# A hand-cut plan of front work over 256 gather groups: new cuts for the early units, and a later due time for a tile's second four heads

## The chip, the cores and the metric

The kernel runs on one core of one Trainium2 chip. The metric is the device time of one execution in microseconds (us), the median of several runs; lower is better.

## The reference, cut to what matters

One layer of a decoder serves a prompt of 1024 rows (8 tiles of 128 rows) and a sample of 8 rows, all in float32. For every row the reference computes

```
h = rmsnorm(x) @ w_in                      # latents, rotary key, three conv inputs
o = softmax(mask(q . k)) @ ckv             # 4 heads, causal; the sample attends to 2048 paged rows
x1 = x + concat(norm(o @ w_uv), norm(conv)) @ w_o
xn2 = rmsnorm(x1)
q = xn2 @ w_query                          # 8 heads x 2 halves x 128
16 best of 128 keys in each half, 16 best of the 256 sums, softmax -> gates, expert numbers
y = rmsnorm(x1 + sum over 128 slots of gate * gelu(xn2 . expert_u[slot]) * expert_v[slot])
```

The last line is the heavy one: each row has 8 x 16 = 128 slots, and each slot wants one row of 4 KB of `expert_u` and one of `expert_v`, fetched by its own number.

## The kernel before, in words

**The stream of groups.** The 128 slots of a tile are served four at a time, so a tile has 32 groups and the 8 prompt tiles have 256. For each slot POOL issues one indirect DMA into `u_ring` and one into `v_ring` (L1853, 128 rows of 4 KB each). Both rings hold 8 slots, which is two groups. In group g, VectorE (DVE) multiplies gelu by the gate (`weigh_group`, L1742) and then takes the four dot products of group g+1 (`dot_group`, L1736); ScalarE (ACT) builds four small diagonal matrices (`diag_group`, L1222) and the gelu of group g+1 (L1215); TensorE (PE) multiplies them with `v_ring` into `acc` (`v_group`, L924, 16 matmuls of 512 columns). A dot product frees its slot of `u_ring`, the matmuls of L924 free theirs of `v_ring`, and only then may POOL gather into that slot again (`gather_group`, L1856). POOL takes the groups in fixed order: the four u gathers of group g+1, the four v gathers of group g.

**The front work.** Everything else (projections, attention, the output projection with `mix_out`, the norms, the queries and the picks of the experts) is cut into named stages. It is done by units: unit 0 is tile 0, unit 1 is tile 1, units 2, 3 and 4 are the pairs of tiles 2 and 3, 4 and 5, 6 and 7, and unit 5 is the sample. The front work of unit 0 runs before the first group; the front work of each later unit runs beside the groups of the tiles before it. `front_of(u)` is projections, attention, feed-forward norm and the query of the first four heads with their `select`; `rest_of(u)` is the query of the last four heads with theirs; in a pair the picks of the second tile are taken later, by `second_picks(u)` (8 `tops` and 2 `select`).

**The plan.** `make_plan` (L178) takes segments (first group, end, list of stages) and lays the stages of a segment over its groups in proportion to the hand-written `COST` (L160). Three engines read the plan: in group g PE does its part of the stages and then `v_group(g)`; DVE does `weigh_group(g)`, `dot_group(g+1)` and then its part of the stages; ACT does `diag_group(g)`, `gelu_group(g+1)` and then its part. In a group with `pages` stages (the sample's attention) the order is a little different: PE puts only the first stage ahead of `v_group`, and DVE puts two of its four dots behind the first stage. POOL and SP don't read the plan: their orders are fixed, and their waits on semaphores follow the stages. SP loads the weights of the stages piece by piece (1 MB each, a ring `w_ring` of two pieces), the tiles of x, and the pages of the sample's cache (32 DMAs for each of 8 samples, double-buffered; the load of one sample waits until the matmuls with the values of the one before the last are done).

**Due times.** `make_plan` asserts that a `select` of tile f lies where a pick buffer is free and before group 32 f - 1. What POOL really waits for (L1856) is finer: the picks of a tile's first four heads before its first group, the picks of the second four heads before its group 16.

Of the kernel before, what the change touches and what calls it, by code (L numbers as in the profile page):

```python
# [44 lines left out]
TOPK = 16  # L45
# [18 lines left out]
G = 4  # L64
GROUPS = SLOTS // G
# [9 lines left out]
SAMPLE = len(UNITS) - 1  # L75
PICK_BUFS = 3
# [17 lines left out]
def parts_of(u):  # L94

    return [(0, 1), (1, 2), (2, 4), (4, 8)] if u == 0 else [(0, 4), (4, 8)]
# [23 lines left out]
def project_stages(u):  # L120

    n = len(UNITS[u])
    return ([(name, i) for i in range(n) for name in ("norm", "turn")] + [("latent", k) for k in range(3)] + [("z_in", 0), ("latent_norm", 0), ("z_in", 1)]
            + [("z_gate", k) for k in range(2)] + [("conv", 0), ("latent_scale", 0), ("conv", 1)] + [("kv_rows", i) for i in range(n)])


def mix_stages(u):

    if u == 0:
        return [(name, 0) for name in ("q_proj", "q_latent", "first_heads", "attn", "first_mix", "first_ffn", "ffn_turn")]  # L130
    stages = []
    for i in range(len(UNITS[u])):
        stages += [("q_proj", i), ("q_latent", i)]
        stages += [("pages", n) for n in range(SB * QUARTERS + QUARTERS)] if u == SAMPLE else [("head", (i, h)) for h in range(H + 1)]
        stages += [("attn", i), ("mix_norm", i)]
    return stages + [("mix_out", k) for k in range(N_OUT)] + [(name, i) for i in range(len(UNITS[u])) for name in ("ffn_norm", "ffn_turn")]


def pick_stages(u, part):

    stages = [("query", 0)] if part == 0 else []
    return stages + [("query", h + 1) for h in range(*parts_of(u)[part])] + [("select", (part, 0))]


def second_picks(u):

    return sum([[("tops", h) for h in range(*heads)] + [("select", (part, 1))] for part, heads in enumerate(parts_of(u))], [])


def front_of(u):  # L150

    return project_stages(u) + mix_stages(u) + pick_stages(u, 0)


def rest_of(u):

    return sum([pick_stages(u, part) for part in range(1, len(parts_of(u)))], [])
# [10 lines left out]
def cost(u, name, n):  # L168

    if name == "head":  # L170
        return 3.5 + 1.2 * UNITS[u][n[0]]
    if name == "select":
        h0, h1 = parts_of(u)[n[0]]
        return 5 + 3 * (h1 - h0)
    return COST[name] * (1.6 if len(UNITS[u]) > 1 and name in SHARED else 1)


def make_plan(segments):  # L178

    groups = [[] for g in range(TILES * GROUPS)]  # L180
    for first, end, stages in segments:
        total, done = sum(cost(*s) for s in stages), 0.0
        for u, name, n in stages:
            g = first + int(done * (end - first) / total)
            if name == "select" and u != SAMPLE:
                f = UNITS[u][n[1]]
                assert f == 0 or max(0, (f + 1 - PICK_BUFS) * GROUPS + 2) <= g < f * GROUPS - 1, (f, g)
            groups[g].append((u, name, n))
            done += cost(u, name, n)
    return [groups[it * GROUPS:(it + 1) * GROUPS] for it in range(TILES)]  # L190
# [16 lines left out]
def of_unit(u, stages):  # L207

    return [(u, name, n) for name, n in stages]


PLAN = make_plan([(0, 30, of_unit(0, rest_of(0)) + of_unit(1, front_of(1) + rest_of(1))),
                  (30, 62, of_unit(2, front_of(2) + rest_of(2))),
                  (62, 74, of_unit(2, second_picks(2))),
                  (74, 120, of_unit(3, front_of(3) + rest_of(3))),
                  (120, 132, of_unit(3, second_picks(3))),
                  (132, 181, of_unit(4, front_of(4) + rest_of(4))),
                  (181, 193, of_unit(4, second_picks(4))),
                  (193, 250, of_unit(SAMPLE, front_of(SAMPLE) + rest_of(SAMPLE) + [("sample_picks", 0)]))])
LAST = TILES - 1  # L220


def has_pages(stages):
    return any(name == "pages" for u, name, n in stages)
# [36 lines left out]
def build(nc, a, out):  # L261

    with ExitStack() as ctx:
# [313 lines left out]
        def _(pe):  # L577
# [407 lines left out]
            def tile(it):  # L985

                for g, stages in enumerate(PLAN[it]):
                    ahead = 1 if has_pages(stages) else len(stages)
# [57 lines left out]
        def _(act):  # L1046
# [210 lines left out]
            def tile(it):  # L1257
                for g, stages in enumerate(PLAN[it]):
                    late = has_pages(stages)
                    if g:  # L1260
                        diag_group(it, g)
                    if g and not late and g + 1 < GROUPS:
                        gelu_group(it, g + 1)
                    if g == GROUPS - 2 and not late and it < LAST:
                        load_xn2(it + 1)
                    for s in stages:
                        stage(own, *s)
                    if g and late and g + 1 < GROUPS:
                        gelu_group(it, g + 1)
                    if g == GROUPS - 2 and late and it < LAST:  # L1270
                        load_xn2(it + 1)
                    if g == X1_GROUP:
                        load_x1(it)
# [31 lines left out]
        def _(dve):  # L1305
# [464 lines left out]
            def tile(it):  # L1770
                for g, stages in enumerate(PLAN[it]):

                    half = G // 2 if has_pages(stages) else G
                    if g:
                        weigh_group(it, g)
                    if g and g + 1 < GROUPS:
                        dot_group(it, g + 1, 0, half)
                    ahead = 1 if has_pages(stages) else len(stages)
                    for s in stages[:ahead]:
                        stage(own, *s)  # L1780
                    if g and g + 1 < GROUPS:
                        dot_group(it, g + 1, half, G)
                    for s in stages[ahead:]:
                        stage(own, *s)
# [167 lines left out]
```

## Time and profile before

| | us |
|---|---|
| median of 3 runs | 3503.11 (3503.08 to 3503.35) |
| the profiled execution | 3499.09 |
| its span, first to last instruction | 3497.3 |
| busy: PE / DVE / ACT / POOL | 2499.0 / 2279.7 / 812.6 / 2290.4 |
| mean granted TensorE clock | 0.842 of full speed |
| bytes moved by DMA, rate over the span | 1279.47 MB, 366 GB/s |

The profile is read by stretches of groups. The start of a group is the start of its multiply of L1742 on DVE. In this trace group 0 starts at 150.2 us, group 8 at 262.5, group 30 at 567.2, group 62 at 1040.4, group 74 at 1181.8, group 120 at 1759.1, group 132 at 1901.6, group 181 at 2524.1, group 193 at 2664.4, group 201 at 2773.2 and group 231 at 3167.8. So 567.2 to 1040.4 is the segment of unit 2's main work (32 groups), 1181.8 to 1759.1 that of unit 3 (46 groups), 1901.6 to 2524.1 that of unit 4 (49 groups), and 2664.4 to 3167.8 the sample's projections and pages. An idle time with an arrow, `<-`, names what ended it.

### The profile page before, as it was taken

How to read it: one execution, taken by the hardware profiler on the slowest of the kernel's cores; microseconds unless marked ns; L12 is line 12 of the kernel's file. 1: busy time of each engine (PE TensorE's matmuls, PEld its weight loads, DVE VectorE, ACT ScalarE, POOL GpSimd, SP SyncE). 2: the span in 40 equal slices, each digit the busy share in tenths (PEclk: the TensorE clock that was granted, in tenths of full speed). 3: DMA queues.
4: the chain of work that ended last, by engine and by line, in shares of the span. 5: the costliest groups of instructions: out<-in, count | busy, mean ns of one | idle time of the engine just before them, and what ended most of it. 6: DMA issues, size and time to landing. Idle time of an engine off the chain costs nothing.

```text
span 3497.3 us, 38783 instructions
## 1 busy us (share of the span) xinstructions
PE 2499.0 (71%) x11520; PEld 1392.1 (40%) x11520; DVE 2279.7 (65%) x5456; ACT 812.6 (23%) x2057; POOL 2290.4 (65%) x2068
## 2 busy tenths in 40 slices
PE   7558775878764598777744978778656978776764
PEld 6425442645531264445311644445213534332321
DVE  3585586655688756657898466558796455554774
ACT  2112212232211212322112223322112122221111
POOL 0366575655657776676777767666676676657675
PEclk8779887999987799899877999889876798987777
DMA  6699999988999999999999999999999999999998
GB/s 237 224 399 363 347 410 334 388 313 298 372 351 372 370 404 371 352 366 412 409 371 372 397 392 349 331 374 410 405 371 379 388 387 370 368 323 394 411 409 338
DMA packets 368936, 1279.47 MB, mean 366 GB/s; under 512 B 59372, under 2 KB 77974, under 8 KB 353368
## 3 DMA queue, kind: packets, MB, share of 16 engines
q0 software_dynamic: 297216, 1082.26, 80.7%
q1 hardware_dynamic: 62324, 168.67, 12.6%
q10 hardware_dynamic: 9188, 26.05, 2.3%
q8 instruction: 95, 1.56, 0.2%
q14 instruction: 113, 0.93, 0.1%
HBM read 1262.31 MB, written 13.48 MB: 365 GB/s over the span
## 4 chain that ended last, share of the span: by engine, by line
DVE 37%; PE 30%; DMA 15%; issue 8%; ACT 4%; SPq 3%; POOL 2%; DVEq 0%; ACTq 0%; POOLq 0%
DVE u_ring L1736 15%; PE acc L924 9%; PE front L586 8%; DMA u_ring<-in_expert_u,pick_cur 7%; DMA v_ring<-in_expert_v,pick_cur 4%; PE front L802 3%; DVE si_u L1603 2%; SPq L536 2%; DVE sv L1602 2%; PE front L711 2%; DVE work L1603 2%; DMA w_ukT<-in_cache_krope 2%; POOL u_ring L1853 1%; DVE work L1602 1%; PE front L734 1%
## 5 line engine op out<-in xcount | busy, mean ns | idle before, releaser
L924 PE MATMUL acc<-v_ring,diag 128*64 128x512 f32 x4096 | 1161.5, 716 | 612.6 <-ACT diag L1222 352.9
L1853 POOL DMA_INDIRECT v_ring<-in_expert_v,pick_cur x1024 | 1133.2, 1107 | 606.1 <-PE acc L924 333.0
L1853 POOL DMA_INDIRECT u_ring<-in_expert_u,pick_cur x1024 | 1140.5, 1114 | 575.4 <-issue 295.1
L1736 DVE CUSTOM_DVE_ANT_0 u_ring<-u_ring,xn_cur 128x1024 f32<-128x1024 f32 x1024 | 1210.8, 1222 | 315.4 <-DMA u_ring<-in_expert_u,pick_cur 309.3
L924 PEld LDWEIGHTS acc<-v_ring,diag 128*64 128x64 f32 x4096 | 340.7, 163 | 1316.6 <-issue 856.9
L1222 ACT ACTIVATE diag<-ident,wgt 128x64 f32<-128x64 f32 x1024 | 272.3, 337 | 797.6 <-DVE wgt L1742 727.9
L586 PE MATMUL front<-work,w_ring 128*128 128x256 f32 (+2 forms) x1536 | 308.1, 343 | 31.0 <-DVE mo L1337 17.1
L586 PE MATMUL front<-mo,w_ring 128*128 128x256 f32 (+2 forms) x1536 | 300.5, 337 | 0.0
L586 PEld LDWEIGHTS front<-work,w_ring 128*128 128x128 f32 x1536 | 250.5, 200 | 83.0 <-issue 29.3
L1215 ACT ACTIVATE gelu<-dots 128x4 f32<-128x4 f32 x256 | 52.5, 205 | 962.9 <-DVE dots L1736 962.8
L586 PEld LDWEIGHTS front<-mo,w_ring 128*128 128x128 f32 x1536 | 255.3, 201 | 23.4
L802 PE MATMUL front<-w_ring,work 128*128 128x256 f32 (+1 forms) x512 | 119.0, 394 | 22.4 <-DVE work L1568 16.7
L1602 DVE MAX8 sv<-work 128x8 f32<-128x128 f32 (+1 forms) x252 | 72.6, 288 | 75.9 <-ACT work L1200 29.9
L802 PEld LDWEIGHTS front<-w_ring,work 128*128 128x128 f32 (+1 forms) x512 | 93.5, 185 | 52.8 <-DVE work L1568 18.5
L1523 DVE COPY rows_next<-front 128x512 f32<-128x512 f32 x32 | 22.1, 691 | 139.7 <-PE front L862 139.7
L1215 ACT ACT_TABLE_LOAD x81 | 103.9, 1283 | 1.5
L734 PE MATMUL front<-work,ckv_rows 128*128 128x128 f32 x560 | 80.3, 307 | 28.7 <-DVE work L1507 25.2
L734 PEld LDWEIGHTS front<-work,ckv_rows 128*128 128x128 f32 x560 | 74.8, 217 | 40.8 <-DVE work L1507 29.5
L1736 DVE DVE_READ_ACCUMULATOR2_ANT dots<- 128x1 f32 x1024 | 84.0, 82 | 0.0
L711 PE MATMUL front<-ckvT,rows_next 128*128 128x512 f32 (+3 forms) x176 | 74.1, 546 | 7.0 <-DVE q_ro L1424 5.9
L1493 DVE SCALAR_TENSOR_TENSOR work<-low_keys,small,front 128x512 f32<-128x512 f32 (+3 forms) x44 | 26.6, 635 | 70.6 <-PE front L712 70.6
L1603 DVE FIND_INDEX8 si_u<-sv,work 128x8 uint32<-128x128 f32 (+1 forms) x252 | 71.5, 284 | 0.6 <-issue 0.6
(303 smaller groups left out, 2374.6 us busy)
## 6 DMA issues: line engine op xcount, KB each, us to landing
w_ring<-in_w_pieces SPq DMA_DIRECT2D x112, 1024.0 KB, 8.4
u_ring<-in_expert_u,pick_cur POOLq DMA_INDIRECT x1024, 10.5
v_ring<-in_expert_v,pick_cur POOLq DMA_INDIRECT x1024, 9.7
x_t<-in_x_prompt SPq DMA_DIRECT2D x16, 512.0 KB
v_ring<-in_w_pieces SPq DMA_DIRECT2D x8, 1024.0 KB, 12.0
work<-in_cache_ckv SPq DMA_DIRECT2D x64, 128.0 KB, 7.9
xn_cur<-scratch ACTq DMA_DIRECT2D x14, 512.0 KB, 9.8
scratch_x<-rows_next ACTq DMA_DIRECT2D x8, 512.0 KB, 6.6
```

What stands on the lines that cost most here:

```text
L536: sp.dma_start(dst, a[src][0, bass.ds(page, 1)].rearrange("a k r -> k (a r)"))\
L586: last = nc.tensor.matmul(dst, w[:, k, c0:c0 + m], x_chunks(k // 4)[:, (k % 4) * T:(k % 4 + 1) * T], start=(k == 0), stop=(k == DC - 1))
L711: nc.tensor.matmul(dst, q_lat[:, c, h, :], ckvT[:, c, ks], start=(c == 0), stop=False)
L734: last = nc.tensor.matmul(F[4][:, c * P:(c + 1) * P], ckv_rows[:, j, c * P:(c + 1) * P], W[1][:, j * P:(j + 1) * P], start=(j == 0), stop= ...
L802: last = nc.tensor.matmul(dst, mixed[i][:, k * T:(k + 1) * T], w[:, k, :], start=(k == 0), stop=(k == DC - 1))
L924: last = nc.tensor.matmul(acc[rows, half, :], diag[:, s % RING, :], v_ring[:, s % RING, half * 512:half * 512 + 512], start=(s < 2), stop= ...
L1215: nc.scalar.activation(gelu[:, g * G:(g + 1) * G], dots[:, g * G:(g + 1) * G], ACT.Gelu).then_inc(on.gelu_done, 1)
L1222: nc.scalar.activation(diag[:, s % RING, :], ident2[:], ACT.Copy, scale=wgt[:, s:s + 1]).then_inc(on.diag_made, 1)
L1602: own(v.max(best, scores), held=True)
L1603: last = v.max_index(index[:, 8 * r:8 * r + 8], best, scores)
L1736: v.tensor_tensor_reduce(u_ring[:, slot, :], u_ring[:, slot, :], xn2_cur[:, block_of(r), :], 1.0, 0.0, ALU.mult, ALU.add, dots[:, g * G + ...
L1853: pool.indirect_dma_start(ring[:, slot, :], None, a[table][0], bass.IndirectOffsetOnAxis(ap=pick, axis=0)).then_inc(loaded[slot], 16)
```

## The change

The due time in the assertion is moved for a tile's second four heads by the 16 groups that lie ahead of their gathers, and the segments are cut anew. The rest of tile 0, the whole of unit 1 and the front of unit 2 (up to its first `select`) become one segment over groups 0 to 61, where before they were two (0 to 29 and 30 to 61, the latter with the rest of unit 2 as well). The rest of unit 2 gets groups 62 to 66. All later segments start later: the 12 groups of each `second_picks` stay 12, unit 3 gets 44 groups for 46, unit 4 48 for 49, the sample 55 for 57.

```diff
             if name == "select" and u != SAMPLE:
                 f = UNITS[u][n[1]]
-                assert f == 0 or max(0, (f + 1 - PICK_BUFS) * GROUPS + 2) <= g < f * GROUPS - 1, (f, g)
+                due = f * GROUPS + parts_of(u)[n[0]][0] * TOPK // G - 1
+                assert f == 0 or max(0, (f + 1 - PICK_BUFS) * GROUPS + 2) <= g < due, (f, g)
...
-PLAN = make_plan([(0, 30, of_unit(0, rest_of(0)) + of_unit(1, front_of(1) + rest_of(1))),
-                  (30, 62, of_unit(2, front_of(2) + rest_of(2))),
-                  (62, 74, of_unit(2, second_picks(2))),
-                  (74, 120, of_unit(3, front_of(3) + rest_of(3))),
-                  (120, 132, of_unit(3, second_picks(3))),
-                  (132, 181, of_unit(4, front_of(4) + rest_of(4))),
-                  (181, 193, of_unit(4, second_picks(4))),
-                  (193, 250, of_unit(SAMPLE, front_of(SAMPLE) + rest_of(SAMPLE) + [("sample_picks", 0)]))])
+PLAN = make_plan([(0, 62, of_unit(0, rest_of(0)) + of_unit(1, front_of(1) + rest_of(1)) + of_unit(2, front_of(2))),
+                  (62, 67, of_unit(2, rest_of(2))),
+                  (67, 79, of_unit(2, second_picks(2))),
+                  (79, 123, of_unit(3, front_of(3) + rest_of(3))),
+                  (123, 135, of_unit(3, second_picks(3))),
+                  (135, 183, of_unit(4, front_of(4) + rest_of(4))),
+                  (183, 195, of_unit(4, second_picks(4))),
+                  (195, 250, of_unit(SAMPLE, front_of(SAMPLE) + rest_of(SAMPLE) + [("sample_picks", 0)]))])
```

Worked out with `make_plan` itself: of the 314 stages in the plan 288 move to another group, each later by one to five groups and none earlier. Some places that the prediction speaks of, before and after:

| stages | group before | group after |
|---|---|---|
| norm of unit 1 to its last select | 8 to 28 | 9 to 30 |
| norm of unit 2, first | 30 | 32 |
| mix_out 0 and 1, mix_out 2 and 3 of unit 2 | 48, 49 | 52, 53 |
| ffn_norm and ffn_turn of tile 2, of tile 3 | 50, 51 | 54 and 55, 55 |
| select of the first, of the second four heads of tile 2 | 56, 60 | 60, 65 |
| first pages stage of the sample | 201 | 202 |
| last stage of the sample | 249 | 249 |

## Rows read from the trace of the kernel before

**Rows 1.** The page: busy time, and what the DMAs moved.
```profile
PE 2499.0 (71%) x11520; PEld 1392.1 (40%) x11520; DVE 2279.7 (65%) x5456; ACT 812.6 (23%) x2057; POOL 2290.4 (65%) x2068
DMA packets 368936, 1279.47 MB, mean 366 GB/s; under 512 B 59372, under 2 KB 77974, under 8 KB 353368
```

**Rows 2.** Busy by stretch: length, PE, PEld, DVE, ACT, POOL, PEclk, DMA share, GB/s.
```profile
262.50:567.20 304.70, 216.78 (x1167) 134.84 (x1169) 209.89 (x527) 72.13 (x183) 191.85 (x168) 0.86 0.96 371
567.20:1040.40 473.20, 368.17 (x1660) 232.32 (x1658) 302.07 (x687) 123.48 (x288) 286.19 (x256) 0.89 0.92 345
1040.40:1181.80 141.40, 65.06 (x194) 19.88 (x192) 127.05 (x363) 26.47 (x75) 106.84 (x97) 0.72 0.97 364
1181.80:1759.10 577.30, 457.98 (x2012) 267.59 (x2010) 378.32 (x821) 146.34 (x367) 405.02 (x370) 0.89 0.99 384
1901.60:2524.10 622.50, 489.84 (x2140) 279.04 (x2138) 397.63 (x848) 159.29 (x387) 438.55 (x393) 0.88 0.98 377
2664.40:2773.20 108.80, 98.71 (x500) 66.65 (x496) 46.48 (x110) 22.43 (x64) 70.87 (x67) 0.70 1.01 403
2773.20:3167.80 394.60, 313.36 (x1675) 149.11 (x1675) 202.66 (x425) 103.16 (x255) 261.96 (x228) 0.87 0.99 360
3167.80:3397.10 229.30, 155.57 (x686) 71.46 (x686) 163.25 (x422) 41.30 (x128) 165.02 (x158) 0.78 1.02 408
```

**Rows 3.** DVE's waits on gathers (total us, times, longest): 567.2 to 1040.4, then 1181.8 to 1759.1.
```profile
DVE u_ring L1736 <- DMA u_ring<-in_expert_u,pick_cur: 17.4, 9, 5.5
...
DVE u_ring L1736 <- DMA u_ring<-in_expert_u,pick_cur: 72.5, 24, 12.7
```

**Rows 4.** Groups of POOL's gathers: busy, mean ns, idle before; the same two stretches.
```profile
L1853 POOL DMA_INDIRECT v_ring<-in_expert_v,pick_cur x128 | 146.6, 1146 | 131.3 <-PE acc L924 99.9 <-issue 31.5
L1853 POOL DMA_INDIRECT u_ring<-in_expert_u,pick_cur x128 | 139.6, 1090 | 55.7 <-issue 36.8 <-DVE dots L1736 18.3 <-PE acc L924 0.6
...
L1853 POOL DMA_INDIRECT v_ring<-in_expert_v,pick_cur x184 | 205.7, 1118 | 104.8 <-PE acc L924 54.4 <-issue 50.3
L1853 POOL DMA_INDIRECT u_ring<-in_expert_u,pick_cur x186 | 200.2, 1076 | 67.8 <-issue 52.8 <-DVE dots L1736 12.9 <-PE acc L924 2.1
```

**Rows 5.** DVE in order of time, groups 48 to 50 (start, length, idle before).
```profile
840.15 0.15 DVE L1742 TENSOR_TENSOR wgt<-gelu,gate_cur 128x4 f32<-128x4 f32 x1
845.16 0.16 DVE L1742 TENSOR_TENSOR wgt<-gelu,gate_cur 128x4 f32<-128x4 f32 x1 [0.27 <-ACT gelu L1215]
850.18 0.16 DVE L1742 TENSOR_TENSOR wgt<-gelu,gate_cur 128x4 f32<-128x4 f32 x1 [0.27 <-ACT gelu L1215]
874.06 1.29 DVE L1578 TENSOR_TENSOR rows_next<-front,x_t 128x512 f32<-128x512 f32 x2 [14.50 <-PE front L802]
```

**Rows 6.** Busy by stretch, L1736 alone: length, DVE busy with its instructions.
```profile
567.20:1040.40 473.20, 150.73 (x256) 0.89 0.92 345
```

**Rows 7.** DVE's waits on gathers: 262.5:567.2, 1901.6:2524.1, 2664.4:2773.2, 2773.2:3167.8; last, PE's on pages.
```profile
DVE u_ring L1736 <- DMA u_ring<-in_expert_u,pick_cur: 10.0, 6, 6.9
...
DVE u_ring L1736 <- DMA u_ring<-in_expert_u,pick_cur: 94.1, 30, 13.3
...
DVE u_ring L1736 <- DMA u_ring<-in_expert_u,pick_cur: 19.9, 6, 7.2
...
DVE u_ring L1736 <- DMA u_ring<-in_expert_u,pick_cur: 12.1, 8, 4.7
PE front L861 <- DMA w_ukT<-in_cache_krope: 29.7, 9, 7.4
```

**Rows 8.** PE in order of time, groups 48 and 49, and a matmul row near group 67.
```profile
840.28 16.14 PE L802 MATMUL front<-w_ring,work 128*128 128x256 f32 x64 [9.30 <-DVE work L1568]
856.36 3.65 PE L924 MATMUL acc<-v_ring,diag 128*64 128x512 f32 x16
859.94 14.08 PE L802 MATMUL front<-w_ring,work 128*128 128x256 f32 x64
...
1127.09 3.68 PE L924 MATMUL acc<-v_ring,diag 128*64 128x512 f32 x8 [7.65 <-ACT diag L1222]
```

## The prediction, made before the changed kernel ran

> **What bounds the kernel now.** First the page. No engine is busy for the whole span: PE 71%, DVE and POOL 65% each [rows 1]. So I went on to the same numbers by stretch [rows 2]. What a reader should see there is the time per group: 473.2 / 32 = 14.8 us in the main segment of unit 2, 304.7 / 22 = 13.9 for unit 1, but 577.3 / 46 = 12.6 for unit 3 and 622.5 / 49 = 12.7 for unit 4, although units 3 and 4 have more attention to do. The early work is packed more tightly, and there the DMAs carry less: 345 GB/s against 384.
>
> Next, who waits for whom. There are two ways to be late. Either the gathers set the pace, and DVE waits for `u_ring`; or the front work does, and POOL waits for slots that PE or DVE haven't freed. In unit 2's stretch DVE waits only 17.4 us for gathers [rows 3], and POOL waits 99.9 + 18.3 = 118.2 us for PE and DVE [rows 4]. In unit 3's it is 72.5 us [rows 3] against 54.4 + 12.9 = 67.3 us [rows 4]. So unit 2 is bound by its chain of stages nearly all the time, and unit 3 about half of it.
>
> Two prices follow. A group in which nothing else happens costs DVE 5.0 us: the starts at 840.15, 845.16 and 850.18 [rows 5], of which 150.73 / 32 = 4.7 are the dots [rows 6]. A group at the pace of POOL costs, in unit 3's stretch, the gathers' busy time and issue gaps without the waits: (205.7 + 200.2 + 50.3 + 52.8) / 46 = 11.1 us [rows 4].
>
> **The change, part by part.** No instruction is added or removed. The new due time only loosens an assertion: it lets the `select` of tile 2's second heads stand in group 65. POOL needs it before group 80, so the wait costs nothing; the cover is 14 groups of gathers, and without it each group of delay would cost POOL 11.1 us. The first `select` of tile 2 moves from 56 to 60. POOL's first u gather of group 64 wants the dots of group 62, which DVE takes in group 61, behind that select; so it isn't late either, but one group later it would be.
>
> The orders on SP and POOL stay as they are. What moves is when their waits end: SP's weight pieces, x tiles and pages follow their stages, later by up to five groups. ACT's stores (latents, x1, xn2) move with them; the one with a reader, xn2 of tile 2, is needed in group 62 and now written in 55 instead of 50. Seven groups hide it. Were that cover gone, DVE would wait for it at the tile change.
>
> What is left is a shift of room. The work of units 0 to 2 gets five groups more (two for 0 and 1, three for unit 2), unit 3 two fewer, unit 4 one fewer, the sample two fewer: one in its projections, one in its pages. The sum of groups is 256 either way, so only the difference between the prices of a group counts. Where the front work is the bound, one more group beside the same work adds the 5.0 us of its own dots. Where POOL is the bound, it adds 11.1. Between them I take the price by the share of the waits that are DVE's:
> - unit 2: 17.4 / (17.4 + 118.2) = 0.13, so 5.0 + 0.13 x 6.1 = 5.8 us.
> - unit 3: 72.5 / (72.5 + 67.3) = 0.52, so 8.2 us.
> - Units 1 and the pages look like unit 2: DVE waits 10.0 us in 22 groups and 12.1 in 30 [rows 7], 0.4 to 0.5 us a group as in unit 2 (17.4 / 32 = 0.5). I take 5.8 for them.
> - Unit 4 and the sample's projections look like unit 3: 94.1 us in 49 groups and 19.9 in 8 [rows 7], 1.9 and 2.5 a group against 1.6. I take 8.2.
>
> The sum: 5 x 5.8 = 29.0 added; 2 x 8.2 (unit 3) + 8.2 (unit 4) + 8.2 (projections) + 5.8 (a group of pages) = 38.6 taken away; **-9.6 us**. The trace doesn't show the price of a group directly, so its bounds are the two ends. Added at 5.0 and removed at 11.1 it is -30; all at one price it is 0; added at 8.2 and removed at 5.0, +16. A check with rows of the profile: between units 2 and 3 14 groups cost 104.1 us, 7.4 each with the extra attention in it, which lies between 5.8 and 8.2.
>
> The even stream does less than it seems to. The worst place of unit 2 stays: two mix_outs in one group keep PE 16.14 and then 14.08 us [rows 8] while DVE runs ahead and then stands 14.5 us [rows 5]. They are still two to a group (52, 53). The feed-forward norms behind them come in one group more. The tile change at group 31, which had norms of unit 2 on both sides, now has none; I put a few us on that and leave them in the range.
>
> **The clock.** PE's granted clock is 0.89 in the crowded stretch and 0.72 in the stretch of second picks, where PE has little to do [rows 2]. [...] Spreading unit 2 thins PE's work, so the mean may fall; but unit 3's, at 0.89 in 46 groups, is already more spread than unit 2's will be. I cost it at nothing; if it fell to unit 1's 0.86, PE's 368 us would grow by 3.5%, 13 us, perhaps half of it on the chain. [...]
>
> **The rivals.**
> - A. Forecast: the prices above, -10 us; its own range -3 to -20. Chance 0.42.
> - B. More: the added groups cost 5.0 and those taken 11.1, or the quieter tile change pays as well: -20 to -32, about 3476. For it: POOL waits for PE or DVE 3.7 us a group in unit 2. Against: two of the groups are taken where DVE hardly waits for gathers, or only half the time. Chance 0.13.
> - C. No change: prices are equal, because the waits belong to single chains (the mix_outs, the norm behind them) and not to crowding, or because DMA is the bound. On DMA: 1279.47 MB [rows 1] at the 408 GB/s of the last full stretch [rows 2] is 3136 us, 10% under the span, so it isn't the bound by these rows. [...] Chance of C 0.21.
> - D. Slower: the stalls of unit 2 stay, since its long chains are kept whole in groups 52 to 55, and the later segments turn crowded. POOL's waits are 118.2 / 32 = 3.7 us a group in unit 2 and 67.3 / 46 = 1.5 in unit 3; over the 14 groups between them the total rises by 3.6 us for each group taken. Five groups taken: 5 x 3.6 = +18 us, 3521. For it: the pages already make PE wait 29.7 us [rows 7], and tighter groups leave SP less time. Against: the first five groups' relief must then be nil. It decides if POOL's waits from unit 2's norm to its last select stay over 110 us. Chance 0.24.
> - That the change doesn't do what it says is excluded for the plan, which the code fixes; for the due time it is true in part, as it changes no instruction.
>
> **How the numbers follow.** The profiled execution took 3499.09 us, 4.0 less than the median of 3503.11. The sum against its own time is 3489.5; against the median, 3493.5. Over 0.2% (7 us, about what a measurement of this kernel can tell from no change) are B and most of A: faster 0.13 + 0.38 = 0.51, rounded up for the tile change to 0.52. Slower is D with what it may have over 7 us: 0.24. The rest, 0.24, is the same. The range takes A, C, most of B and two thirds of D: 3474 to 3516.
>
> **What would show it.** In the changed kernel, from unit 2's first norm to its last select (groups 32 to 66), the time should be about 473 + 17 = 490 us and POOL's waits for PE and DVE fall from 118 toward 105; unit 3's 44 groups should take about 577 - 16 = 561 us, unit 4's 48 about 614, pages 389. DVE's wait for gathers in unit 3 should fall from 72.5 to near 65. I am wrong if unit 2's stretch takes over 500 us (the added groups came at POOL's price), or if units 3 and 4 don't get shorter by more than 15 us together (they were bound by their chains). A fall of the clock in unit 2 below 0.87 would be the clock's share.

## The result, and the profile after

| | before | after |
|---|---|---|
| median of 6 runs | 3503.22 us (3502.58 to 3510.40) | 3482.93 us (3478.57 to 3492.61) |
| the profiled execution, its span | 3499.09, 3497.3 | 3482.97, 3481.2 |

The ratio is 0.9943, with a 95% interval of 0.9926 to 0.9960. Measured a second time, among the experiments below, it was 0.9968 (0.9955 to 0.9981), with medians of 3487.23 and 3500.24. The change is worth 0.3 to 0.6%, 11 to 20 us. The forecast was 3493.5 us, 10 less than before, with a range of 3474 to 3516.

The page of the changed kernel, the two lines that answer to [rows 1]:
```profile
PE 2504.6 (72%) x11520; PEld 1399.3 (40%) x11520; DVE 2277.3 (65%) x5456; ACT 823.2 (24%) x2065; POOL 2291.3 (66%) x2068
DMA packets 368936, 1279.47 MB, mean 368 GB/s; under 512 B 59372, under 2 KB 77974, under 8 KB 353368
```
The same work is done: the same bytes, the same count of matmuls, the busy times within 1.5%. Only waiting has gone. So, as before, the reading goes by stretches. The busy time by stretch of the changed kernel, columns as in [rows 2]; groups 32 to 66 (unit 2), unit 3, unit 4, its second picks, the sample up to group 230, groups 231 to 249:
```profile
593.50:1076.80 483.30, 373.73 (x1700) 229.63 (x1702) 313.62 (x711) 134.19 (x309) 309.22 (x276) 0.90 0.95 360
1211.30:1773.50 562.20, 441.68 (x1980) 260.12 (x1978) 368.42 (x804) 149.66 (x362) 389.70 (x355) 0.89 0.99 380
1913.80:2514.50 600.70, 477.01 (x2126) 275.24 (x2123) 392.88 (x839) 156.75 (x381) 426.94 (x386) 0.90 1.00 387
2514.50:2655.20 140.70, 62.46 (x194) 18.63 (x192) 126.79 (x363) 26.48 (x76) 107.91 (x97) 0.75 1.00 375
2655.20:3154.20 499.00, 411.60 (x2131) 219.49 (x2127) 238.06 (x510) 124.46 (x310) 317.52 (x281) 0.79 0.97 355
3154.20:3384.40 230.20, 168.38 (x700) 78.43 (x702) 162.46 (x425) 41.30 (x128) 163.54 (x156) 0.74 1.03 410
```
And its waits, as in [rows 3] and [rows 4]: three lines for unit 2's 35 groups, three for unit 3's 44, three for unit 4's 48, and last two of the kernel before, POOL's waits in unit 4's 49. The columns are total us, times, longest.
```profile
POOL v_ring L1854 <- PE acc L925: 77.6, 25, 10.1
DVE u_ring L1737 <- DMA u_ring<-in_expert_u,pick_cur: 45.6, 12, 11.9
POOL u_ring L1854 <- DVE dots L1737: 21.2, 5, 7.0
...
DVE u_ring L1737 <- DMA u_ring<-in_expert_u,pick_cur: 61.6, 23, 7.9
POOL v_ring L1854 <- PE acc L925: 58.6, 30, 17.3
POOL u_ring L1854 <- DVE dots L1737: 14.9, 6, 5.0
...
DVE u_ring L1737 <- DMA u_ring<-in_expert_u,pick_cur: 83.8, 33, 8.5
POOL v_ring L1854 <- PE acc L925: 53.8, 27, 6.9
POOL u_ring L1854 <- DVE dots L1737: 9.4, 4, 3.8
...
POOL v_ring L1853 <- PE acc L924: 63.6, 33, 10.5
POOL u_ring L1853 <- DVE dots L1736: 8.8, 2, 5.0
```
What to see: in unit 2 POOL waits 98.8 us in 35 groups, where it waited 118.2 in 32, and DVE now waits 45.6 us for gathers instead of 17.4. The crowded stretch has become less bound by its chain. Unit 3, with two groups fewer, lost 11 us of DVE's waits and gained 6 of POOL's. In unit 4 both kinds of wait fell, DVE's from 94.1 [rows 7] to 83.8 and POOL's from 72.4 to 63.2. A lost group alone doesn't explain that: less room should make POOL wait more, as in unit 3.

Two traces of each kernel (the second ones are from the experiments) give the balance by stretch. A stretch is taken from the start of a group to the start of another, with the second picks in the unit that they belong to:

| stretch | before, two traces | after, two traces | difference of means | predicted |
|---|---|---|---|---|
| up to group 8 | 262.5, 258.3 | 258.5, 259.4 | -1.5 | 0 |
| units 1 and 2 (66 groups; 71 after) | 919.3, 921.1 | 952.8, 956.6 | +34.5 | +29.0 |
| unit 3 (58; 56) | 719.8, 718.4 | 702.5, 704.1 | -15.8 | -16.4 |
| unit 4 (61; 60) | 762.8, 763.5 | 741.4, 742.8 | -21.1 | -8.2 |
| sample up to group 231 (38; 36) | 503.4, 507.8 | 499.0, 496.4 | -7.9 | -14.0 |
| from group 231 | 329.5, 327.9 | 327.0, 326.8 | -1.8 | 0 |
| sum | 3497.3, 3497.0 | 3481.2, 3486.1 | -13.5 | -9.6 |

The two rows of the sample don't hold quite the same work. Before, the sample's pages stand in groups 201 to 230; after, in 202 to 231, so that their last stage falls into the row "from group 231". Taken up to the end of the pages, 38 groups took 503.4 and 507.8 us before, and 37 took 510.8 and 508.1 after. The groups behind the pages, up to 249, took 229.4 and 227.5 us before (19 of them), and 218.4 and 218.1 after (18).

### The profile page after: what moved, and what is told of

Its sections match the earlier page's. It is cut to its first block, busy times and chain, and to the rows that moved or that the text cites. A ratio compares the mean times of both kernels' runs of the same rounds, so it can differ in the third digit from the quotient of the medians.

```text
span 3481.2 us, 38789 instructions
## 1 busy us (share of the span) xinstructions
PE 2504.6 (72%) x11520; PEld 1399.3 (40%) x11520; DVE 2277.3 (65%) x5456; ACT 823.2 (24%) x2065; POOL 2291.3 (66%) x2068
## 4 chain that ended last, share of the span: by engine, by line
DVE 36%; PE 35%; DMA 13%; issue 7%; ACT 4%; POOL 2%; SPq 2%; DVEq 0%; ACTq 0%; POOLq 0%
DVE u_ring L1737 14%; PE acc L925 11%; PE front L587 10%; DMA u_ring<-in_expert_u,pick_cur 6%; PE front L803 3%; DMA v_ring<-in_expert_v,pick_cur 2%; DVE si_u L1604 2%; DVE sv L1603 2%; PE front L712 2%; PE front L735 2%; DVE work L1604 2%; DMA w_ukT<-in_cache_krope 1%; DVE work L1603 1%; DVE work L1648 1%; DVE work L1650 1%
## 5 line engine op out<-in xcount | busy, mean ns | idle before, releaser
L925 PE MATMUL acc<-v_ring,diag 128*64 128x512 f32 x4096 | 1176.1, 723 | 623.1 <-ACT diag L1223 354.7
L925 PEld LDWEIGHTS acc<-v_ring,diag 128*64 128x64 f32 x4096 | 347.8, 165 | 1328.7 <-issue 905.6
L1603 DVE MAX8 work<-mo 128x8 f32<-128x256 f32 (+1 forms) x144 | 61.4, 426 | 15.5 <-DVE mo L1625 0.9
```

What stands on the lines that cost most here:

```text
L925: last = nc.tensor.matmul(acc[rows, half, :], diag[:, s % RING, :], v_ring[:, s % RING, half * 512:half * 512 + 512], start=(s < 2), stop= ...
L1603: own(v.max(best, scores), held=True)
```

## The experiments

Two theories were set against each other. **Prices**, that of the prediction: a group taken or given is worth 5.0 to 11.1 us, by how crowded its stretch is. **Places** (called layout once it had taken shape): what counts is where single heavy stages fall, against the tile change or against each other. All ratios are to runs of the kernel before on the same chip, as they stand in the record. The quotient of two printed medians can lie up to 0.0013 away from the ratio: for the run with the old cut at group 30 it is 0.9955, and the ratio 0.9968.

**Both kernels again.** The first is the changed kernel with nothing altered.

> The changed kernel again, nothing altered, for a second trace. It says how far a single stretch moves between two executions of the same program. Both theories expect about 3483 us and each stretch within 3 us of the first trace of the changed kernel (groups 8 to 31: 334.9; 32 to 66: 483.4; unit 3: 562.2; unit 4: 600.7; pages 402.8). If stretches move by more than 5 us, readings of single stretches below that size are worth nothing.

Measured: 3487.23 us, ratio 0.9968 (0.9955 to 0.9981). Its stretches are in the table: within 4 us of the first trace everywhere. The kernel before again:

> The kernel before again, nothing altered, for a second trace of it. Both theories expect the stretches of the first trace within 3 us (groups 8 to 61: 777.9; unit 3: 577.4; unit 4: 622.6), except the sample's projections and pages (503.4), which the trace with the merged segment alone had at 493.1 with the same plan there.

One run, 3498.88 us, no interval. Stretches within 2 us from group 8 up to the sample (up to group 8 it is 4 us), whose projections and pages took 507.8 against 503.4. With the trace of the next experiment that is 493.1 to 507.8 for one and the same plan, so a reading of the sample's stretch is good to 7 us at best. For the others 4 us looks enough here, but groups 8 to 66 of the changed plan, in six traces, took from 818 to 829 us.

**The merging alone.**
```diff
-PLAN = make_plan([(0, 30, ... rest_of(0), front_of(1) + rest_of(1)),
-                  (30, 62, of_unit(2, front_of(2) + rest_of(2))),
+PLAN = make_plan([(0, 62, ... rest_of(0), front_of(1) + rest_of(1), front_of(2) + rest_of(2)),
                   (62, 74, of_unit(2, second_picks(2))),
```


> The merging alone: units 0, 1 and 2 in one segment over groups 0 to 61 with the rest of unit 2 in it, everything later as before the change. No group of room changes hands. The theory of prices (a group's price follows from how crowded its stretch is) expects no change from before: 3503 +- 5 us. The theory of places (what counts is where heavy stages fall against the tile change at group 31 and against each other) expects part of the gain here, 5 to 10 us, so 3493 to 3498.

3497.97 us, ratio 1.0000 (0.9984 to 1.0016). Groups 8 to 61 took 775.1 us against 777.9 and 779.0. By the costs of the table `COST` the two old segments were almost equally full already, so the even stream moves five stages, by one group each. It is worth nothing that can be measured; the quieter tile change, on which I had put a few us, is in that nothing.

**The old cut at group 30, with the new room.**
```diff
-PLAN = make_plan([(0, 62, ... units 0 and 1, front_of(2)),
+PLAN = make_plan([(0, 30, ... units 0 and 1),
+                  (30, 62, of_unit(2, front_of(2))),
                   (62, 67, of_unit(2, rest_of(2))),
```


> The changed kernel with the first segment cut in two again: units 0 and 1 over groups 0 to 29 as before the change, the front of unit 2 over 30 to 61, its rest in 62 to 66; later segments as in the changed kernel. Unit 1 gives its two extra groups back and unit 2 has five more than before. The theory of prices, with 5.8 us for a group in either, expects the changed kernel's time, 3483 +- 4. The theory of places says that unit 1's two groups cost 15 us each (304.7 to 334.9) for no relief: with them back in unit 2 it expects 3465 to 3475.

3484.55 us, ratio 0.9968 (0.9947 to 0.9988), the changed kernel's own. The busy time by stretch, groups 8 to 29 and 30 to 66:
```profile
257.90:563.70 305.80, 224.56 (x1167) 139.00 (x1169) 209.64 (x526) 72.39 (x183) 190.00 (x168) 0.83 0.95 370
563.70:1083.00 519.30, 396.38 (x1740) 239.98 (x1738) 328.93 (x741) 135.90 (x322) 332.38 (x298) 0.88 0.95 358
```
Together 825.1 us, against 818.3 and 822.1, and the total is the one that prices expected, not the 3465 to 3475 of places. It doesn't matter, within what can be measured, whether the five groups go to unit 2 alone or two of them to unit 1. The reading "15 us for each of unit 1's two groups" was an error of bookkeeping: in the changed plan the tile change at group 31 counts with unit 1, before with unit 2.

**Five groups that relieve nothing.**
```diff
                   (62, 74, of_unit(2, second_picks(2))),
-                  (74, 120, of_unit(3, front_of(3) + rest_of(3))),
+                  (79, 123, of_unit(3, front_of(3) + rest_of(3))),
...
```


> The kernel before up to group 73, then five groups (74 to 78) with no front work, then the later segments exactly as in the changed kernel. It measures what five groups cost where they relieve nothing, and what the later segments give by losing five. The theory of prices expects the later segments to give what they gave in the changed kernel's trace (about 47 us from unit 3 on) and the idle groups to cost POOL's pace, 5 x 10.2 to 11.1 = 51 to 56 us: 3507 to 3512. If the idle groups cost only DVE's 5 us each, it would be 3481, and the room of unit 2 would be worth nothing in itself.

3501.80 us, ratio 1.0009 (0.9991 to 1.0026). The idle groups 74 to 78, then unit 3:
```profile
1180.90:1226.00 45.10, 22.84 (x72) 6.44 (x68) 25.19 (x45) 6.35 (x25) 35.04 (x34) 0.80 0.99 381
1226.00:1796.70 570.70, 450.86 (x1990) 264.60 (x1992) 368.98 (x803) 149.79 (x362) 393.30 (x361) 0.88 0.98 381
```
The five cost 45.1 us themselves, 9.0 each, and unit 3 after them took 7.7 more (570.7 against 562.2 and 563.8 in the changed kernel): behind the idle groups DVE has no gathers in hand any more, and group 79 alone took 18.0 us instead of 12.7, with a wait of 4.7 us for a gather where the changed kernel has none. That is 52.8 us, 10.6 a group: POOL's pace, as expected. The same five groups given to units 1 and 2 cost 34.5. So putting the room to use, rather than leaving it idle, is worth about 18 us by the traces and 14 by the two ratios (1.0009 and 0.9968), and without a use for it the later savings are just paid back: no gain. This run shows one half of the forecast's mechanism, that a group with work to relieve costs less than POOL's pace. It doesn't show the other half, that a group taken from unit 3 or 4 gives back more than a group given to unit 2 costs.

**Unit 4 with its 49 groups, three groups later.**
```diff
-                  (135, 183, of_unit(4, front_of(4) + rest_of(4))),
-                  (183, 195, of_unit(4, second_picks(4))),
-                  (195, 250, of_unit(SAMPLE, ...
+                  (135, 184, of_unit(4, front_of(4) + rest_of(4))),
+                  (184, 196, of_unit(4, second_picks(4))),
+                  (196, 250, of_unit(SAMPLE, ...
```


> The changed kernel, but unit 4 keeps its 49 groups (135 to 183), its second picks 184 to 195, the sample 54 groups (196 to 249). Unit 4 then has exactly the layout of stages on groups that it had before, three groups later against the tile change at group 160. The three traces of the changed later segments had it at 601 to 602 us with 48 groups, before it was 622.6 with 49. The theory of prices expects 601.5 + 8.2 = about 610. The theory of places expects 600 to 604 if the 21 us came from attn and mix_norm of tile 7 standing right at the tile change, and 620 or more if they came from the layout within the unit. Total: prices about the changed kernel's time, +-4.

3501.89 us, ratio 0.9995 (0.9983 to 1.0006): one group moved, and the whole gain is gone. Unit 4's stretch:
```profile
1927.70:2548.30 620.60, 488.36 (x2140) 279.39 (x2138) 397.85 (x849) 155.62 (x384) 438.89 (x393) 0.89 0.99 381
```
620.6 us, against 600.7 with 48 groups. So the tile change is not it, and a step of 20 us is far more than the price of 8.2. What changed with one group is which stages share a group. With 49, `make_plan` puts latent_scale and conv together, and attn and mix_norm of both tiles, and leaves 8 groups empty; with 48 none of the three pairs falls together, and 4 groups are empty. The total rose more than this stretch: in this trace groups 8 to 66 took 828.6 us as well, against 818.3 and 822.1 in the two traces of the changed kernel, and I have no cause for that.

Here is what a pair costs, in the traces of before and after. In each of the two windows the same stages are on the same number of groups. First before: groups 141 to 144 (one empty, latent_scale with conv, one tile's kv_rows, the rest up to q_latent), then groups 149 to 151 (the last head, one empty, attn with mix_norm):
```profile
2007.60:2067.50 59.90, 42.49 (x190) 24.99 (x189) 34.05 (x60) 7.51 (x26) 40.97 (x39) 0.86 1.03 411
2118.30:2155.80 37.50, 30.05 (x163) 17.67 (x159) 23.65 (x37) 10.77 (x23) 29.05 (x26) 0.91 0.96 343
```
And after, one stage to a group, groups 144 to 147 and 152 to 154:
```profile
2023.60:2077.40 53.80, 35.85 (x167) 19.46 (x166) 34.28 (x61) 7.62 (x26) 37.95 (x36) 0.87 1.03 410
2128.20:2162.00 33.80, 28.73 (x163) 17.15 (x159) 23.20 (x38) 10.88 (x23) 25.96 (x24) 0.95 0.95 346
```
59.9 to 53.8 and 37.5 to 33.8: 9.8 us with DVE's work the same (34.1 and 34.3, 23.7 and 23.2). The trace of DVE shows how. Before, group 150 is empty and still takes from 2123.57 to 2130.24:
```profile
2123.57 0.16 DVE L1742 TENSOR_TENSOR wgt<-gelu,gate_cur 128x4 f32<-128x4 f32 x1
2130.24 0.16 DVE L1742 TENSOR_TENSOR wgt<-gelu,gate_cur 128x4 f32<-128x4 f32 x1 [1.94 <-ACT gelu L1215]
2139.96 1.23 DVE L1555 TENSOR_TENSOR work<-mo 128x1024 f32<-128x1024 f32 x1 [0.74 <-ACT mo L1167]
2144.78 1.29 DVE L1315 TENSOR_SCALAR work<-front 128x512 f32<-128x512 f32 x2 [3.60 <-PE front L790]
2149.63 1.23 DVE L1310 TENSOR_TENSOR work<-work 128x1024 f32<-128x1024 f32 x1 [3.56 <-ACT work L1050]
```
And after, groups 153 and 154:
```profile
2144.81 1.23 DVE L1556 TENSOR_TENSOR work<-mo 128x1024 f32<-128x1024 f32 x1 [6.59 <-ACT mo L1168]
2150.63 1.28 DVE L1316 TENSOR_SCALAR work<-front 128x512 f32<-128x512 f32 x2
2155.78 1.22 DVE L1311 TENSOR_TENSOR work<-work 128x1024 f32<-128x1024 f32 x1 [3.88 <-ACT work L1051]
```
Before, in the one group that holds both stages, DVE waits 3.60 us for PE's sums and then 3.56 for ACT's reciprocal root, with nothing of its own to put there; in groups 150 and 151 it also waits 3.8 us for gathers, 1.94 for gelu and 0.74 for ACT's copy of attention's sums (`mo`): 13.7 us in all. After, with attn and mix_norm in groups of their own, the four dots of a group lie in front of the sums, L1316 starts without a wait, and no wait for gathers is left in the two groups; the wait for the root stays (3.88 us). Not everything got better: the wait for ACT's copy grew from 0.74 to 6.59 us, where before an empty group stood between the last head and attn. Together DVE waits 10.5 us, 3.2 less than before.

The other traces agree. The second window took 37.5 to 38.7 us in all six traces in which unit 4 has 49 groups, and 32.5 to 34.2 in the eight with 48 or 46. The first took 59.9 to 62.4 in those six, and 53.7 to 59.2 in the seven with 48. The third pair, attn and mix_norm of tile 7, shows it where the group numbers are equal: groups 160 to 163 took 51.0 us in this experiment's run and 45.1 and 45.5 in the changed kernel. But with everything two groups later, as in the last two experiments, the same four groups took 51.4 and 53.4 us with the pair apart, no less than the 50.9 with the pair together in the experiment before them. So where a pair stands matters as well.

**The same from the other side: before, with 48 groups for unit 4.**
```diff
-                  (132, 181, of_unit(4, front_of(4) + rest_of(4))),
-                  (181, 193, of_unit(4, second_picks(4))),
+                  (132, 180, of_unit(4, front_of(4) + rest_of(4))),
+                  (180, 192, of_unit(4, second_picks(4))),
                   (193, 250, of_unit(SAMPLE, ...
```


> The kernel before, with unit 4's main segment cut from 49 groups to 48 (132 to 179) and its second picks in 180 to 191; group 192 has no front work, everything else stands where it stood. With 49 groups the plan puts latent_scale and conv, and twice attn and mix_norm, into one group, beside 8 empty groups; with 48 none of these three pairs falls together and 4 groups are empty. The theory of layout expects unit 4's stretch at 601 to 603 us in place of 622.6, the idle group at 9 to 10, so 11 us under the time before, ratio 0.997. The theory of prices (a group is worth 5 to 8.2 us) expects 614 to 617 and the time before, ratio 1.000.

3488.36 us, ratio 0.9971 (0.9954 to 0.9989). Unit 4, its second picks, the idle group 192:
```profile
1899.60:2504.50 604.90, 484.26 (x2124) 279.10 (x2122) 393.06 (x840) 157.89 (x382) 430.60 (x385) 0.89 0.99 382
2504.50:2647.40 142.90, 69.31 (x200) 20.53 (x196) 130.06 (x367) 22.56 (x72) 112.40 (x101) 0.70 0.99 365
2647.40:2652.30 4.90, 1.19 (x4) 0.59 (x6) 1.83 (x7) 3.89 (x8) 3.68 (x5) 0.50 1.02 407
```
752.7 us for the same 61 groups that took 762.8 and 763.5. One segment boundary, moved by one group and with the group left idle, gives as much as the second measurement of the whole change (0.9968). The 10.5 us are a net sum: unit 4's stretch gave 18 us, and the second picks with the idle group took back 7.5. The 18 hold the price of the group as well as the layout. The idle group took 4.9 us and not the 9 to 10 expected.

**And with 46**, also a layout without those three pairs, though other stages share a group in it that had one each with 48.
```diff
-                  (132, 180, ...), (180, 192, ...),
+                  (132, 178, of_unit(4, front_of(4) + rest_of(4))),
+                  (178, 190, of_unit(4, second_picks(4))),
```


> The same with 46 groups for unit 4 (132 to 177), its second picks in 178 to 189, three groups idle. With 46 groups the layout again has none of the three pairs, and 3 empty groups, so that this run against the one with 48 gives the price of a group with the layout held still. Theory of layout with the prices of the prediction: 601.5 - 2 x 8.2 = 585 us for the stretch; if the groups taken relieved nothing it would be 601.5 - 2 x 11.1 = 579; if the unit is then bound by its chain, 601.5 - 2 x 5.0 = 591. Total: two idle groups more at 9 to 10 us, so within 5 us of the run with 48.

3493.90 us, ratio 0.9981 (0.9967 to 0.9996).
```profile
1902.60:2489.40 586.80, 467.29 (x2092) 272.00 (x2090) 383.24 (x822) 156.57 (x373) 408.80 (x369) 0.90 0.99 378
```
604.9 - 586.8 = 18.1 us for two groups, 9.0 each. With these pairs apart in both, the price is near the forecast's 8.2. The total came out 5.5 us above the run with 48: unit 4, its second picks and the idle groups together took 757.3 us, against 752.7. The step from 49 to 48 was 18 us (622.6 to 604.9) and 20 us (620.6 to 600.7): by this price 9 for the group and 9 to 11 for the layout. The three windows above would give the layout 10 to 17 us and the group the rest, so the split between the two is not sharp.

**Room from the idle end.** First before, with the sample's segment made four groups longer.
```diff
-                  (193, 250, of_unit(SAMPLE, ...
+                  (193, 254, of_unit(SAMPLE, ...
```


> The kernel before with one number changed: the sample's segment ends at group 254 instead of 250, so it has four groups more, taken from the six groups without front work at the end. The theory of prices expects four groups more at 5.8 to 8.2 us (+28), and four idle ones less at 10.2 (-41): 13 us under the time before, ratio 0.996. If the pages keep their own clock (the loads of one sample after the other), extra groups lengthen the sample's stretch little, and the gain is 25 to 40 us, ratio 0.989 to 0.993. If the end of the kernel (picks of the sample, its loads, its last gathers) is late instead, it is 0 or a loss.

3494.21 us, ratio 0.9977 (0.9965 to 0.9989), a gain of 8 us; the prices had said 13. The sample's 41 groups up to the end of its pages took 531.3 us, against 503.4 and 507.8 for 38, so 8.6 a group and not 5.8: the pages have no pace of their own, and room isn't cheap there. The figure is rough, 7.8 to 9.3 by which of the two traces is taken. Then the changed kernel's first 79 groups with units 3 and 4 at their old sizes and everything ending three groups later:
```diff
-                  (79, 123, ...), (123, 135, ...), (135, 183, ...), (183, 195, ...), (195, 250, SAMPLE)
+                  (79, 125, ...), (125, 137, ...), (137, 186, ...), (186, 198, ...), (198, 253, SAMPLE)
```


> The changed kernel's first 79 groups, then units 3 and 4 with the 46 and 49 groups that they had before, and the sample's 55 groups ending at 253 instead of 250. The room for units 0 to 2 is taken from the idle end instead of from units 3 and 4. Against the changed kernel the theory of prices expects unit 3 +16, unit 4 +8, and three idle groups less, -31: 6 us under the changed kernel, ratio to before 0.995. If unit 4 needs 620 us with this layout wherever it stands, it loses 12 more: ratio 0.998 to 1.000.

3480.74 us, ratio 0.9944 (0.9922 to 0.9966), as the prices had it, although unit 4 took 620.0 us with its 49 groups, as the layout had it. Its profiled execution was its slowest, 3499.19 us; so only the stretch is read from that trace, and not the total.

**A version meant to beat both**: the same, but unit 4 with the 48 groups of the good layout and the sample with 56.
```diff
-                  (137, 186, ...), (186, 198, ...), (198, 253, SAMPLE)
+                  (137, 185, ...), (185, 197, ...), (197, 253, SAMPLE)
```


> The changed kernel's first 79 groups, unit 3 with 46 groups, unit 4 with the 48 of the good layout, the sample with 56 groups ending at 253. Against the run that ended at 253 with 49 groups for unit 4 (3480.7 us, ratio 0.9944) the theory of layout expects -20 for unit 4 and +7 for one group more of the sample: about 3468, ratio 0.990 to 0.992. The theory of prices expects no difference: 0.994.

3474.78 us (3468.46 to 3484.93), ratio 0.9934 (0.9914 to 0.9955). The lowest median of the study, though short of the 0.990 to 0.992 expected. Its interval overlaps the changed kernel's first one and the last run's too (0.9922 to 0.9966), so the totals don't show that it is better than either. Unit 3, unit 4 and unit 4's second picks:
```profile
1211.70:1785.30 573.60, 454.25 (x2012) 261.15 (x2010) 379.15 (x822) 151.55 (x371) 406.27 (x371) 0.89 0.99 388
1927.90:2530.00 602.10, 478.02 (x2122) 275.75 (x2120) 394.76 (x839) 154.22 (x379) 420.36 (x386) 0.90 1.00 386
2530.00:2677.10 147.10, 64.00 (x194) 19.53 (x192) 126.79 (x362) 26.47 (x75) 108.14 (x97) 0.71 0.98 359
```
602.1 us for unit 4 where the last run had 620.0: the layout again, as far as one trace of each can tell. Ending two groups later still:

> The same with the sample's segment ending at 255, so 58 groups, its last stage in group 254 and only group 255 without front work. Two idle groups at 10.2 us are given up for two groups of the sample at about 7: 6 us less, about 3462, ratio 0.989, if the end of the kernel still hides the sample's own gathers and loads. If those come late, its last stretch (from group 255 on, 42.2 us before) grows and the gain is lost: 3468 or more.

3475.50 us, ratio 0.9937 (0.9920 to 0.9953): no further gain. The part from group 255 took 48.9 us, against 42.2 in the first traces of before and after, and DVE's longest wait there for the sample's own gathers grew from 9.9 to 16.6 us: they begin to come late.

## Why the prediction was right, and where it wasn't

**The total was right in good part by luck.** The forecast took its 9.6 us from a difference of prices: 5.8 for a group given to units 1 and 2, 8.2 for one taken from unit 3 or 4. The two kernels' own traces give 34.5 / 5 = 6.9 and 15.8 / 2 = 7.9. All traces with these plans give 952.5 to 963.8 us for the early units after (six traces) and 919.2 to 923.1 before (six), on average 37 us or 7.4 a group; and for unit 3 702.5 to 705.0 after (four) and 715.5 to 720.0 before (six), on average 14.8 us, also 7.4 a group. So no difference between these two prices is shown. What stood in for it was the layout of unit 4, which the forecast didn't have. Take it away, as the changed kernel with 49 groups for unit 4 does, and the ratio is 0.9995: no gain (some 8 us of that lie in groups 8 to 66, whose longer time there has no cause yet). Give it alone, as the kernel before with 48 does, and it is 0.9971.

**What bounds the kernel** stood in part. Idle groups cost 10.6 us each, where 11.1 was forecast for POOL's pace, and groups with work to relieve cost 7.4. This difference is real, and the run that took its room from the idle end shows it: 0.9944 with unit 4 still in its bad layout.

**Units 1 and 2.** Predicted +29.0, measured +34.5. The forecast for groups 32 to 66 was 490 us; it took 483.3 and 486.8 us. The first tile change had moved out of it, to the groups up to 31, and the second in from the second picks, which fell from 141.4 to 134.5. POOL's waits fell to 98.8, and to 105.8 in the second trace; 105 was forecast.

**Unit 3.** Predicted -16.4, measured -15.8; the stretch forecast at 561 took 562.2, and DVE's waits, forecast near 65, were 61.6; in the second trace they were 70.2.

**Unit 4.** Here a term was mis-sized: predicted -8.2, measured -21.1. The step that failed is "Unit 4 and the sample's projections look like unit 3", with its 8.2. It treated a segment as evenly filled. The price of the group itself was about 9.0; the rest, 9 to 12 us by that price, goes with which stages `make_plan` happens to put together, and that I could have read from the plan before the run: three pairs and 8 empty groups before, none and 4 after.

**The sample.** Predicted -14.0, measured -7.9 up to group 231, with 7 us of scatter on one plan, and -9.7 with what follows. One of its two terms stood for a group that wasn't taken where the forecast took it. The pages have 30 groups before (201 to 230) and 30 after (202 to 231); the second group is lost behind them, where 19 became 18. Up to the end of the pages the time rose by 3.9 us with one group fewer, where 8.2 were to be saved; behind them, up to group 249, it fell by 10.2. The forecast for the pages alone, 389 us, assumed 29 groups; the 30 took 414.6 us, with q_latent in group 202 as well. Nor did the price of 5.8 for a group of pages show anywhere: with four groups more the sample's stretch gave 8.6.

**The even stream and the due time.** The first was given a few us and is worth none (ratio 1.0000). The due time cost no wait for picks: from 1185 to 1232 us, around the first gathers of group 80, POOL's longest wait is 0.3 us. The select in group 65 did hold up one gather into `u_ring`: it waited 5.06 us, until 1073.91, for dots that DVE takes behind that select. From 1055.8 to 1088 us DVE's dots waited for no gather.

**The clock.** 0.90 in unit 2's stretch after, 0.89 before [rows 2]: no loss there. But PE was as busy per us as before, 373.7 / 483.3 against 368.2 / 473.2, so this stretch doesn't test whether thinner work of PE lowers its clock; no run here shows that it does. Two stretches of the kernel before had nearly the same low clock with PE busy for very different shares: 0.72 with 65.1 of 141.4 us, 0.70 with 98.7 of 108.8 [rows 2]. In the sample's stretch the clock did fall: up to the end of the pages it was 0.82 or 0.83 in five traces with the plan of before, and 0.79 and 0.80 in the two of the changed kernel; two other runs with its plan there had 0.80 (the old cut at group 30) and 0.82 (the five idle groups). The forecast put the clock at nothing everywhere; what this cost no run separates.

**The rivals.** Slower (D) was to be decided by POOL's waits over 110 us in unit 2's stretch; they were 98.8 and 105.8. No change (C) fell as a total, with the interval, and its DMA bound with the 410 GB/s of the last stretch. Its other reason, equal prices because the waits belong to single chains, is what the runs show for units 2 and 3, and for the pairs of unit 4. The first measurement (-20 us) lies at the edge of B, the second (-13) in A. B's reasons were wrong: the even stream with its quieter tile change was worth nothing, and the groups added cost 7.4 us and not 5.0. What put the result there was the layout, which no rival named. Two errors, unit 4 by -13 and the early units and the sample by +5 and +6, partly cancelled. The total was better than its parts, and that is luck.

What stays open: why groups 8 to 66 took 829 us in two traces (and 825 in one) and 818 to 822 in three others of the same plan; why the sample takes no less time up to the end of its pages with one group fewer; and whether splitting the pairs of stages in a whole segment, at an unchanged number of groups, gives the same 10 us. In each run here the pairs and the number of groups changed together; only the windows above hold the count of groups still, and other stages changed groups as well.

## What to carry to other kernels

Where a hand-cut plan runs beside a stream of fixed pace, look first for room that lies idle. Groups without front work, several together, cost 10.2 to 10.6 us each here, and one more group for the same work about 7.4; between two working stretches the sums of waits promised a difference of 2.4 us a group, and none showed. Then print the plan: a proportional split with rounding can put two long-latency stages into one slot beside an empty one, and moving one such boundary by one group was worth as much here (0.9971) as the whole change in its second measurement. Test a new cut with its room left idle, as a control, before believing where a gain comes from.

## What the runs showed of the hardware that was not expected

The DMAs held 410 GB/s over 230 us (groups 231 to 249 after). POOL, unhindered, issues an indirect gather every 1.24 us, as two rows of it in order of time, from the end of the changed kernel, show:
```profile
3399.08 0.94 POOL L1854 DMA_INDIRECT u_ring<-in_expert_u,pick_cur  x1 [0.30 <-issue]
3400.32 0.94 POOL L1854 DMA_INDIRECT u_ring<-in_expert_u,pick_cur  x1 [0.30 <-issue]
```
Eight gathers are 9.9 us, and groups 252 to 254, without front work, take 10.2: there the issue of the gathers is as near a limit as the DMAs, whose busy share over these groups is 1.03, at 410 GB/s. And one plan gave totals from 3485 to 3511 us over 31 runs of the kernel before, against 3502.6 to 3510.4 in its first six: a single time of this kernel says nothing about 0.3%.
